# Static orders of VectorE, PE and ScalarE laid anew around the second projection pass

## The reference, cut to what matters

```python
def hybrid_mixer(xn, w_in, b_gates, w_dw, ...):
    p = xn @ w_in                       # q, k, v, o, gates, a, g
    gates = p[..., 4*W:4*W + 2*H] + b_gates
    ...                                 # mLSTM in chunks, with log_sigmoid(f) summed along the tokens
    u = a * sigmoid(g)
    c = depthwise_conv(full) + b_dw     # 31 taps
    c = silu(group_norm(c, gn_gain, gn_bias))
    out = concatenate([h, c]) @ w_out

def peer_ffn(xn, w_query, keys1, keys2, u_tab, v_tab):
    ...                                 # top 16 of 128 x 128 product keys, 8 heads: 128 experts a token
    u_sel = u_tab[experts]
    act = gelu(einsum('nd,nhkd->nhk', xt, u_sel))
    z = gate * act
    return einsum('nhk,nhkd->nd', z, v_tab[experts])
```

## Time and profile before

| | us |
|---|---|
| median of 3 runs | 1828.65 |
| lowest and highest run | 1823.42, 1835.83 |
| the profiled execution, its own time | 1838.51 |
| its span in the profile | 1836.8 |
| mean granted TensorE clock | 0.751 |

### The profile page before, as it was taken

The page is one execution under the profiler, slowest core; times in us unless marked ns, Lnnn a source line. Parts: engine busy times, 40 slices in busy tenths (PEclk is TensorE's granted clock), DMA queues, the critical chain, the costliest instruction groups (busy, mean ns, idle before and its releaser), DMA issues.

```text
span 1836.8 us, 16626 instructions
## 1 busy us (share of the span) xinstructions
PE 1126.5 (61%) x5557; PEld 554.4 (30%) x5557; DVE 1056.7 (58%) x2708; ACT 273.1 (15%) x660; POOL 1087.9 (59%) x1194
## 2 busy tenths in 40 slices
PE   8866999887777789783343367543333344333345
PEld 8864544355654675450000011100000000000001
DVE  5454867747465584766565774565656565744420
ACT  3332245312210242220000000000000000000000
POOL 5523446645545555456766666666666666666764
PEclk9887999998878899895665678765555565665567
DMA  8776699979998999999999999999999999999997
GB/s 276 290 259 257 227 363 375 395 296 333 404 344 302 347 355 395 357 376 367 384 370 361 363 376 391 372 373 368 370 369 367 370 378 363 371 380 369 371 366 278
DMA packets 178652, 643.92 MB, mean 351 GB/s; under 512 B 21728, under 2 KB 21736, under 8 KB 178440
## 3 DMA queue, kind: packets, MB, share of 16 engines
q0 software_dynamic: 156672, 570.49, 80.5%
q1 hardware_dynamic: 21320, 70.28, 10.5%
q10 hardware_dynamic: 576, 2.10, 0.3%
HBM read 637.24 MB, written 5.16 MB: 350 GB/s over the span
## 4 chain that ended last, share of the span: by engine, by line
PE 29%; DVE 19%; POOL 18%; issue 15%; another core or an unknown queue 13%; DMA 5%; ACT 2%; ACTq 0%; DVEq 0%; POOLq 0%
PE pp L769 11%; POOL ring L726 9%; DVE ring L1244 5%; PE pp L779 5%; PE y L1061 4%; POOL w_ring L726 3%; POOL C_sample L726 2%; POOL act_T L726 2%; DMA ring<-in_u_experts,expert_idx 1%; DVE w_ring L1244 1%; DVE lists L1573 1%; DVE C_sample L1244 1%; PE a L1061 1%; POOL keys_T L726 1%
## 5 line engine op out<-in xcount | busy, mean ns | idle before, releaser
L726 POOL DMA_INDIRECT ring<-in_u_experts,expert_idx x348 | 330.3, 949 | 364.6 <-remote 110.4
L1244 DVE SCALAR_TENSOR_TENSOR ring<-ring,x_normed 128x1024 f32<-128x1024 f32 x348 | 411.8, 1215 | 106.5 <-DMA ring<-in_u_experts,expert_idx 79.9
L726 POOL DMA_INDIRECT ring<-in_v_experts,expert_idx_by_token x323 | 311.1, 963 | 183.0 <-issue 84.5
L769 PE MATMUL pp<-act_T,w_ring 128*128 128x128 f32 (+2 forms) x1200 | 262.1, 380 | 27.1 <-issue 13.2
L1061 PE MATMUL a<-ring,z_columns 128*32 128x512 f32 x604 | 228.2, 935 | 53.5 <-issue 36.9
L1061 PE MATMUL y<-ring,z_columns 128*32 128x512 f32 x760 | 225.6, 766 | 35.6 <-issue 22.8
L769 PEld LDWEIGHTS pp<-act_T,w_ring 128*128 128x128 f32 x1200 | 184.1, 203 | 108.3 <-issue 98.4
L1061 PE MATMUL a<-act_T,z_columns 128*32 128x512 f32 x112 | 87.9, 1033 | 145.0 <-DMA ring<-in_v_experts,expert_idx_by_token 122.4
L1061 PE MATMUL y<-act_T,z_columns 128*32 128x512 f32 x92 | 67.8, 901 | 88.2 <-DMA ring<-in_v_experts,expert_idx_by_token 70.8
L779 PE MATMUL pp<-w_ring,act_T 128*128 128x128 f32 (+1 forms) x832 | 111.2, 296 | 10.1 <-issue 3.8
L779 PEld LDWEIGHTS pp<-w_ring,act_T 128*128 128x128 f32 (+1 forms) x832 | 104.7, 191 | 23.0 <-issue 17.4
(11 more groups left out here) (356 smaller groups left out, 1928.6 us busy)
## 6 DMA issues: line engine op xcount, KB each, us to landing
w_ring<-in_w_all SPq DMA_DIRECT2D x99, 512.0 KB
ring<-in_u_experts,expert_idx POOLq DMA_INDIRECT x348
ring<-in_v_experts,expert_idx_by_token POOLq DMA_INDIRECT x323
ring<-in_w_all SPq DMA_DIRECT2D x8, 512.0 KB, 9.5
x_res<-in_x_prompt SPq DMA_DIRECT2D x4, 512.0 KB, 6.5
C_sample<-in_state_C SPq DMA_DIRECT2D x4, 512.0 KB
out_C_s<-C_sample ACTq DMA_DIRECT2D x4, 512.0 KB
out_y_p<-x_res SPq DMA_DIRECT2D x16, 128.0 KB
```

The lines of the kernel that those rows point to most:

```text
L726: pool.indirect_dma_start(out=slot[s], out_offset=None, in_=a["u_experts"] if kind == "u" else a["v_experts"], in_offset=bass.IndirectOffs ...
L769: ins = pe.matmul(p[:, lo:width], w[:, k, :], actT[:, k, lo:width], start=(k == 0), stop=(k == KC - 1))
L1244: dve.scalar_tensor_tensor(out=slot[s], in0=slot[s], scalar=1.0, in1=xn_now[:, :], op0=ALU.mult, op1=ALU.mult, accum_out=dots[:, part % 4, ...
```

## The change

The three orders are laid anew; no instruction is added or dropped, and from the point of `conv_sample(0)` on, by which both have done 131 steps, VectorE's order is as before. What VectorE does at the points that change (d: dot, r: a step of routing, g: gates of a part):

| between | before | after |
|---|---|---|
| `root1` and `gate_rows(1)` | 17 d, r | 15 d, r, d |
| `gate_rows(1)` and `gated(1, first)` | d r d r r r, 5 d | 5 d, r r r r, 3 d |
| `gated(1, first)` and `gated(1, second)` | 12 d, g, 3 d | 12 d, g, 7 d |
| `gated(1, second)` and `rows_after(1)` | d | d |
| `taps(0)` and `taps(1)` | 11 d, r, 3 d, r | 7 d, r, 3 d, r |
| `taps(1)` and `exponents(2)` | d d r d r r, 4 d, r, 5 d, r, g, d | r d r r, 7 d, r, 4 d, r, g, d |
| `taps(2)` and `keys_weighted(2)` | 9 d, 3 r | 10 d, 3 r |
| `carried(2)` and `centre` 0 | 6 d | 5 d |
| `centre` 2 and `centre` 3 | 3 d | 4 d |
| `scale` 0 and `scale` 1 | 4 d, g | 3 d, g, d |
| `scale` 2 and `scale` 3 | d | none |
| state (L1510) and output (L1520) of `new_state(2)` | none | d |
| `conv_sample(0)` and `residual_early(0)` | d d | d |

So `gated(1, second)`, `rows_after(1)` and `taps(0)` come behind four more dots than before. On PE v group 14 runs between L924 and L930 of `within_chunk(2)` instead of behind the last `var` job of "rest". On ScalarE the gates of part 2 come one job earlier: in front of the evacuation of v projection 22 instead of behind it.

```diff
--- before.py
+++ after.py
@@ -215,22 +215,22 @@
-DVE_STEPS = ("r8 d17 r1 d1 r1 d1 r3 d17 g1 d15 r1 d3 r1 d2 r1 d1 r2 d4 r1 d5 r1 g1 d3 r1 d3 r1 d1 r1 d25 g1 d22 r1 "
-             "d1 r1 d1 r1 d1 r2 d5 g1 r5 d34 g1 d22 r1 d1 r1 d1 r1 d1 r2 d7 f1 d1 g1 d1 r1 d3 r1 d1 r1 d1 r1 d2 r1 "
-             "d6 r1 d5 r1 d1 r1 d3 r1 d2 r1 d6 g1 d1 r1 d5 r1 d1 r1 d3 r1 d3 r1 d19 g1 d1 r1 d5 r1 d1 r1 d3 r1 d3 "
-             "r1 d19 g1 d1 r1 d6 r1 d1 r1 d2 r1 d3 r1 d3 f1 d16 g1 d1 r1 d5 r1 d1 r1 d3 r1 d3 r1 d3 f1 d16 g1 d1 "
-             "r1 d6 r1 d1 r1 d3 r1 d2 r1 d19 g1 d1 r1 d5 r1 d1 r1 d3 r1 d3 r1 d19 g1 d1 r1 d5 r1 d2 r1 d2 r1 d3 r1 "
-             "d19 g1 d1 r1 d5 r1 d1 r1 d3 r1 d3 r1 d3 f1 d16 g1 d32 g1 d30 g1")
+DVE_STEPS = ("r8 d15 r1 d6 r4 d15 g1 d15 r1 d3 r2 d1 r2 d7 r1 d4 r1 g1 d4 r1 d2 r1 d2 r1 d24 g1 d22 r1 d1 r1 d1 r1 "
+             "d1 r2 d5 g1 r5 d34 g1 d22 r1 d1 r1 d1 r1 d1 r2 d7 f1 d1 g1 d1 r1 d3 r1 d1 r1 d1 r1 d2 r1 d6 r1 d5 r1 "
+             "d1 r1 d3 r1 d2 r1 d6 g1 d1 r1 d5 r1 d1 r1 d3 r1 d3 r1 d19 g1 d1 r1 d5 r1 d1 r1 d3 r1 d3 r1 d19 g1 d1 "
+             "r1 d6 r1 d1 r1 d2 r1 d3 r1 d3 f1 d16 g1 d1 r1 d5 r1 d1 r1 d3 r1 d3 r1 d3 f1 d16 g1 d1 r1 d6 r1 d1 r1 "
+             "d3 r1 d2 r1 d19 g1 d1 r1 d5 r1 d1 r1 d3 r1 d3 r1 d19 g1 d1 r1 d5 r1 d2 r1 d2 r1 d3 r1 d19 g1 d1 r1 "
+             "d5 r1 d1 r1 d3 r1 d3 r1 d3 f1 d16 g1 d32 g1 d30 g1")
...
-    0, 0, 0, 8, 26, 37, 53, 54, 70, 89, 89, 101, 101, 101, 101, 107, 107, 111, 115, 118, 119, 124, 128, 128, 129,
-    129, 129, 129, 131, 131, 132, 132, 133, 133, 133, 133, 135, 135, 137, 138, 140, 144, 145, 145, 146, 155, 155,
+    0, 0, 0, 8, 25, 37, 57, 58, 70, 89, 89, 102, 102, 102, 102, 107, 107, 111, 115, 119, 120, 125, 129, 129, 129,
+    129, 130, 130, 131, 131, 132, 132, 133, 133, 133, 133, 135, 135, 137, 138, 140, 144, 145, 145, 146, 155, 155,
...
-    10, 11, 11, 12, 12, 12, 13, 13, 14, 14, 14, 14, 15, 16, 16, 16, 16, 17, 17, 17, 17, 17, 17, 17, 17, 18, 18, 18,
+    10, 11, 11, 12, 12, 12, 13, 13, 14, 14, 15, 15, 15, 16, 16, 16, 16, 17, 17, 17, 17, 17, 17, 17, 17, 18, 18, 18,
...
-    2, 2, 2, 3, 3, 3, 3, 3, 3, 3, 3, 3, 3, 3, 3, 3, 3, 3, 3, 3, 3, 3, 3, 3, 3, 3, 3, 3, 3, 3, 3, 3, 3, 4, 4, 4, 4,
+    2, 2, 3, 3, 3, 3, 3, 3, 3, 3, 3, 3, 3, 3, 3, 3, 3, 3, 3, 3, 3, 3, 3, 3, 3, 3, 3, 3, 3, 3, 3, 3, 3, 4, 4, 4, 4,
...
```

## The result

| | before | after |
|---|---|---|
| median, us | 1827.28 (20 runs) | 1839.95 (20 runs) |
| lowest and highest run | 1821.54, 1835.83 | 1833.15, 1845.90 |
| the profiled execution, its own time | 1838.51 | 1840.12 |
| its span in the profile | 1836.8 | 1838.4 |

The ratio is 1.0061, 95% interval 1.0048 to 1.0075, which is 9 to 14 us slower; the medians lie 12.7 us apart. I had forecast 1827.2, no measurable change. 1839.95 is just inside the range (1814 to 1840), but on the side, and by a step, that I had not forecast.

A forecast was written before the change was run, and what follows sets the result against it. The mixer's chain (PE 29%, VectorE 19%, unexplained 13%) sets the pace first, transfers bound the long last stage. Terms 0 + 0 + 0 + 0 + 0 - 1.4 take the median from 1828.65 to 1827.2 us; range 1814 to 1840.

The forecast's parts named there:

- 13% of unexplained pieces: Mixer's chain: pieces where an engine stood still and nothing in the profile let it go, 13% of the chain.
- taps(1) to exponents(2): Routing put ahead of dots there: same work up to the 64th dot, cost 0, bounds 0 and 1.5 us.
- the hole in the gathers at 280 to 288 us: Price of routing first: some 3 to 4 us without gathers, taken up by 11 us free in the next stretch.
- My cover: PE's v group 4 could wait up to 1.5 us; PE's wait for ScalarE right behind it covers that.
- The four dots: Before gated(1, second): 4.56 us of dots fit VectorE's 4.84 us wait for ScalarE; cost and gain 0, bound 4.56.
- Ahead of gated(1): Dots and routing reordered before gated(1, second): VectorE's waits for ScalarE hide it; cost 0, 2.2 us to spare.
- taps(2) to centre(3): One dot more or less at points where VectorE idles or waits for PE, which sets the pace: cost 0.
- Gates of part 2: ScalarE's part one job earlier: gates at about 409.7, scale 1 2.8 us earlier, lost in idle time before normalise(2); gain 0.
- v group 14: PE, moved in front of L930: 1.92 us of work beside VectorE's normalise; cost 0, bounds -1.67 and +1.92 us.
- The rival that the group delays `normalise(2)`: At within_chunk(2): VectorE is let go by var 3, not dens; +1.92 us, gain not seen, 1830.6 us; chance 0.12.
- The -1.4 at the end: Dots around new_state(2): earlier gathers let v group 16 start at 456.5 to 457.1, gain 1.1 to 1.7, taken as 1.4 us.
- A piece more falls on the chain: Rival: unexplained pieces are dealt out anew and one more, 9.9 us, joins the chain: 1837.2 us; chance 0.13.

The follow-up runs named there:

- first_half: Kernel before with only the edits ahead of taps(1), four more dots among them: 1.0007 on a chip with the waits, 0.9986 on one without.
- second_half: Kernel before with routing first between taps(1) and exponents(2) and all edits behind taps(2): 1.0063 on a chip with the waits (before 1828.13 us).
- four_dots_alone: Kernel before with seven dots instead of three behind gates of part 0, seven instead of eleven behind taps(0): 0.998 on a chip without the waits.

## Why the prediction was wrong

**What bounds the kernel.** I read 13% of unexplained pieces off the chain and treated them as scatter that lies over the work. By the record they are late updates of the kernel's own counters; they are in all traces of the slower kind of chip, where the kernel takes 195 us more, and in none of the other; and they answer to the orders (0.03 against 8 to 13 us at the second L2015). All the other steps rested on this one.

**"taps(1) to exponents(2): cost 0, bounds 0 and 1.5".** This is the step that failed: 12 to 13 us on a chip with the waits (1.0073), nothing on the others (1.0003, 0.9992, 1.0002). My reason for the 0 was that ScalarE waits for the 64th dot there, and PE behind ScalarE. With routing first ScalarE was late by itself: its L2015 went on 12.9 us behind the PE job that it waits for, the copies behind it took 9.05 us, and its gates came at 310.43 without a wait for a dot, 9.8 us later than in `first_half`. I had seen the hole in the gathers at 280 to 288 us and asked only when the lost transfers are made up. I had not asked what the old pause at 286 to 289 us did for the engines, nor what a run of gathers without one does to them. My cover, "PE stood waiting for ScalarE right behind that group", failed too: the group itself grew from 1.9 to 8.9 us in `second_half`. By the bound alone nobody could have come above 1.5 us, because it was taken from a landing, and what is late here are updates of counters. That the edit costs the 12 to 13 us rests on one set of runs on one chip (5 of it, 8 of before), and that the first delay is seen at this place on three traces. Why updates come late, and how the loss gets from there to the end, stays open: in the pair of traces most of it comes behind 438 us.

**The four dots: 0, bound 4.56.** What they stand in front of came 4.5 us late in the trace after, but VectorE still waited 5.59 us for ScalarE there, which had stood 3.82 us without a named releaser; and, as said, it cost nothing: `taps(1)` at 272.87, first half 1.0007. On chips without the waits the part gains 3 us (0.998), which my sum did not have.

**Ahead of gated(1), taps(2) to centre(3).** 0 forecast; 0.9994 measured for the first, and for all behind `taps(2)` 1.0007 and 0.9991. Right within what can be told, on chips without the waits; on one with them only `first_half` (1.0007) speaks for the first, and nothing for the second.

**Gates of part 2.** Gain 0 was right, the way to it was not quite: no wait at 412.65, 3.1 us earlier, but VectorE stood 1.96 us in front of `scale` 1, which began at 417.48 and not 2.8 us earlier. The gain is gone there, and not only in front of `normalise(2)`.

**v group 14: 0, with -1.67 and +1.92 as bounds.** `normalise(2)` did begin at 434.10, which I had named as a sign that I am wrong. But VectorE's row in `second_half`, which has the group moved too:

```profile
433.29 0.17 DVE L1477 TENSOR_TENSOR n_prompt<-n_prompt,decay 128x4 f32<-128x4 f32 x1 [4.47 <-PE pp L924]
```

It is let go by L924, that is by `dens`, and not by the job behind it. The rival that the group delays `normalise(2)` by standing in front of it falls; 0 was right for that. The trace agrees here with the Trainium skill (TensorE: Matmul & The Clock Gate, on packing small matmuls, the mechanism), that a signal on the last matmul of a job is sound; the row at 432.06 that seemed to differ begins 1.67 us behind the end of `dens` (430.39), and I count it among the late updates.

**The -1.4 at the end** was not seen by itself: v group 16 began 1.0 us later, not 1.1 to 1.7 earlier. The whole change gained 2.3 us on a chip without the waits, and the half ahead of `taps(1)` alone gains as much there (0.9986).

**The rivals.** "A piece more falls on the chain: 1837.2", to which I gave 0.13, is the nearest in number and in kind. That it is one piece more is not shown: the delays at the second L2015, and those behind 438 us, are several. I had held against it that all behind is the same stream at the same places, and that few instructions are fetched. The Trainium skill (Runtime: NRT & Kernel Launch, on instruction fetch mechanics) says that the cost of crossing into a new block of code is mostly hidden. The queue's row is 45 packets and 0.74 MB in `four_dots_alone` as in the earlier trace rows, so the amount of code fetched is not what sets the two kinds of chip apart. Nor is it the transfer of a packet: the 45 took 43.2 us together in the trace of before and 43.0 in `four_dots_alone`. Whether they were asked for late, no run here shows. What I should have done is to weigh a range of this size as a property of the order of the gathers, not as luck.

## What to carry to other kernels

Where a chain has a large share of waits without a releaser, find out which counter each waits for and when the instruction that raises it ended: here ScalarE stood up to 13.0 us behind a job of PE that was done. Then measure the same kernel on other chips and at other times before pricing an edit: here these waits went with 195 us of 1828, were absent elsewhere, and the edit's cost was seen only with them. Then look at the pauses of the densest transfer queue as well as at its speed: an edit that took away a pause of 3 us by making the one ahead of it longer went with ScalarE standing for 18 us and a group of PE's stretched from 1.9 to 8.9. And what a local wait is worth shows only in the median at the end: 6.5 us won at 310 us were 0.1 at 607 and 4.1 at 896, and the median was no better.

## What the runs showed that I had not expected

- The same kernel takes 1633 us on most chips met and 1828 or 1847 us on others, one chip number in both groups, with the same transfers at nearly the same best rate (418 GB/s over 16 us in the trace of before, 419 over 720 us in `four_dots_alone`), but with less than half of the counters' updates on record in the slower. What sets the kind was not found.
- Where it is slower, GpSimd stands about 5 us at every 32nd gather of the last stage, whatever the kernel, and mostly at the same numbers (617, 649, 681 and so on, counted from 0). In `first_half` the 18 of these waits from gather 457 to 1001 add up to 93 us, beside the 95 by which that stretch is longer than without them (815.6 against 720.2).
- Besides these, VectorE stands up to 11.4 us and ScalarE, at L2015, up to 18.1 us for counters of the kernel's own engines, and PE inside jobs that have no wait. What makes the updates late was not found.
